# Moving the row fetch between weight pairs, and loading the first pair as two transfers, in a mixture-of-experts decoder step

## The reference

```
proj  = h @ w_in                                  # (tokens, 1024) @ (1024, 3072)
mixed = stick_breaking_attention | differential_attention
x     = layer_norm(ALPHA * x + mixed @ w_out)
logits = x @ w_router + b_router                  # 32 experts
gates  = softmax(top_4(logits))
for the tokens routed to expert e:
    g, u = split(x @ w_gate_up[e] + b_gate_up[e]) # (n, 1024) @ (1024, 2048)
    hid  = (clip(u, -7, 7) + 1) * (min(g, 7) * sigmoid(1.702 * min(g, 7)))
    y   += gate * (hid @ w_down[e] + b_down[e])   # (n, 1024) @ (1024, 1024)
x     = layer_norm(ALPHA * x + y)
```

## Time and profile before

| | |
|---|---|
| median of 3 runs | 1326.35 us (1326.22 to 1326.98) |
| profiled execution, its own time | 1327.01 us |
| its span, first to last instruction | 1325.2 us |
| mean granted TensorE clock | 0.987 |
| PE busy | 1271.4 us (96%) |
| DVE busy | 457.1 us (34%) |
| ACT busy | 260.4 us (20%) |
| moved by DMA | 498.38 MB, mean 376 GB/s |
| PE idle until gate and up weights land (L1815) | 11.5 us |

### The profile page before, as it was taken

How to read it: one execution, slowest core, us unless ns; L and a number is a source line. 1 busy time by engine, 2 the same in 40 slices (tenths; PEclk the granted TensorE clock), 3 DMA queues, 4 the chain that set the end, 5 groups by cost and what they waited for, 6 DMA issues and landing times.

```text
span 1325.2 us, 19517 instructions
## 1 busy us (share of the span) xinstructions
PE 1271.4 (96%) x7682; PEld 514.0 (39%) x7683; DVE 457.1 (34%) x986; ACT 260.4 (20%) x607; POOL 85.5 (6%) x92
## 2 busy tenths in 40 slices
PE   8999997999999999999999999999999999999995
PEld 6354444664433333333333333333333333333332
DVE  1265364775842232222332222233222232222225
ACT  1333345753420110100110100011100110100002
POOL 2023234310010000000000000000000000000000
PEclk9999998999899999999999999999999999999998
DMA  9679779887589999999999995999999999999992
GB/s 367 243 292 355 253 312 372 303 357 256 199 313 409 426 429 428 428 428 427 430 429 428 428 428 234 406 426 428 430 428 428 428 429 428 428 430 429 427 428 93
DMA packets 53308, 498.38 MB, mean 376 GB/s; under 512 B 6793, under 2 KB 7945, under 8 KB 26386
## 3 DMA queue, kind: packets, MB, share of 16 engines
q1 hardware_dynamic: 41586, 430.62, 77.9%
q0 software_dynamic: 11520, 67.11, 13.1%
q10 hardware_dynamic: 160, 0.07, 0.0%
HBM read 493.58 MB, written 3.93 MB: 375 GB/s over the span
## 4 chain that ended last, share of the span: by engine, by line
PE 50%; DMA 23%; ACT 2%; DVE 1%; issue 0%; SPq 0%; ACTq 0%; DVEq 0%
PE psum L1815 25%; DMA arena<-in_w_gate_up 23%; PE psum L1863 11%; PE psum L1461 4%; PE psum L1796 3%; PE psum L1644 2%; PE psum L1476 2%; PE psum L1469 1%; ACT arena L1945 1%; ACT arena L1979 1%; PE psum L1628 1%; PE psum L1667 0%; PE psum L1656 0%; DVE arena L2353 0%; PE psum L1639 0%
## 5 line engine op out<-in xcount | busy, mean ns | idle before, releaser
L1815 PE MATMUL psum<-arena 128*64 128x512 f32 x2112 | 462.2, 593 | 11.5 <-DMA arena<-in_w_gate_up 11.5
L1815 PEld LDWEIGHTS psum<-arena 128*64 128x64 f32 x2112 | 150.4, 137 | 316.0 <-issue 288.4
L1863 PE MATMUL psum<-arena 128*64 128x512 f32 x1056 | 233.9, 595 | 3.3
L2296 DVE TENSOR_SCALAR arena<-psum 128x512 f32<-128x512 f32 x33 | 22.8, 692 | 610.6 <-PE psum L1815 610.6
L1863 PEld LDWEIGHTS psum<-arena 128*64 128x64 f32 x1056 | 72.9, 137 | 150.2 <-issue 131.9
L2243 DVE SCALAR_TENSOR_TENSOR arena<-psum,arena 128x1024 f32<-128x1024 f32 (+1 forms) x96 | 103.3, 1103 | 69.4 <-PE psum L1800 37.2
L1975 ACT ACTIVATE arena<-arena 128x512 f32<-128x512 f32 x32 | 20.2, 630 | 455.4 <-DVE arena L2296 455.4
L1461 PE MATMUL psum<-arena 128*64 128x512 f32 x408 | 95.1, 601 | 0.0
L1191 DVE STREAM_TRANSPOSE arena<-arena 128x1024 f32<-128x1024 f32 x64 | 75.0, 1217 | 1.8 <-DVE arena L1291 0.9
L1796 PE MATMUL psum<-arena 64*128 64x512 f32 x264 | 65.9, 615 | 1.9 <-issue 1.9
L1983 ACT ACTIVATE arena<-psum 128x512 f32<-128x512 f32 x33 | 19.7, 597 | 239.8 <-PE psum L1863 239.8
(11 more groups left out here) (268 smaller groups left out, 1001.0 us busy)
## 6 DMA issues: line engine op xcount, KB each, us to landing
arena<-in_w_gate_up SPq DMA_DIRECT2D x128, 2048.0 KB, 19.6
arena<-in_w_down SPq DMA_DIRECT2D x62, 2048.0 KB, 16.6
arena<-in_w_in SPq DMA_DIRECT2D x12, 1024.0 KB, 11.8
arena<-in_w_out SPq DMA_DIRECT2D x4, 1024.0 KB, 10.6
arena<-in_w_down SPq DMA_DIRECT2D x4, 1024.0 KB, 13.9
arena<-in_x_prompt SPq DMA_DIRECT2D x4, 512.0 KB, 5.0
out<-arena SPq DMA_DIRECT2D x8, 256.0 KB, 6.3
arena<-in_ln_g SPq DMA_DIRECT2D x2, 512.0 KB, 7.6
```

The source lines that it names most:

```text
L1815: ins = nc.tensor.matmul(psum[64 * h:64 * h + 64, n, :], x_k, slot[k][:, col:col + 512], start=False, stop=(k == KD - 1))
L1863: ins = nc.tensor.matmul(psum[64 * h:64 * h + 64, 7, :], h_k, slot[s][:, col:col + 512], start=(k == 0), stop=(k == KD - 1))
```

## The change

The fetch of the next item's rows moves, in every item but item 0, from behind slot 7 to between slot 3 and slot 4. The first pair (slots 0 and 1) becomes two transfers of 1 MB. Each has its own `w_loaded` and `w_used` semaphore; the even rows (8 KB pieces, one for each partition, 16 KB apart in memory) go to slot 0 and the odd rows to slot 1, so each slot holds what it held before. SP issues them in the order 0, 1, 2, 4, 6, 8, 10. The other pairs stay as they are.

```diff
+HALVED = (0,)
-        w_loaded = {s: sem(f"w_loaded{s}") for s in range(0, RING, 2)}
+        w_loaded = {s: sem(f"w_loaded{s}") for s in range(RING) if s % 2 == 0 or s - 1 in HALVED}
             if s < KD:
-                src = a["w_gate_up"][0, bass.ds(e, 1), s * P:(s + 2) * P, :].rearrange("e (p r) n -> (e p) (r n)", r=2)
-                dst = ring[:, s * SLOT:(s + 2) * SLOT]
+                first = s // 2 * 2
+                rows = a["w_gate_up"][0, bass.ds(e, 1), first * P:(first + 2) * P, :]
+                if first in HALVED:
+                    src = rows.rearrange("e (p r) n -> r (e p) n", r=2)[s % 2]
+                    dst = slot[s]
+                else:
+                    src = rows.rearrange("e (p r) n -> (e p) (r n)", r=2)
+                    dst = ring[:, s * SLOT:(s + 2) * SLOT]
@@ SP, before the items
-                load_weights(sp, 0, 0)
+                for s in (0, 1):
+                    load_weights(sp, 0, s)
-        w_used = {s: sem(f"w_used{s}") for s in range(0, RING, 2)}
+        w_used = {s: sem(f"w_used{s}") for s in range(RING) if s % 2 == 0 or s - 1 in HALVED}
+        products_done = w_used[KD - 1 if KD - 2 in HALVED else KD - 2]
@@ SP, expert 1
-                for s in range(0, KD, 2):
-                    sp.wait_ge(w_used[s], done)
-                    load_weights(sp, 1, s)
+                for s in w_used:
+                    if s < KD:
+                        sp.wait_ge(w_used[s], done)
+                        load_weights(sp, 1, s)
@@ SP, experts 2 to 31
-                    for s in range(0, RING, 2):
+                    for s in w_used:
                         sp.wait_ge(w_used[s], done)
                         load_weights(sp, e, s)
@@ PE, body(t)
                     for k in range(KD):
-                        if k % 2 == 0:
+                        if k in w_loaded:
                             pe.wait_ge(w_loaded[k], loaded)
...
-                        if k % 2:
+                        if k in w_used and k // 2 * 2 in HALVED:
+                            ins.then_inc(w_used[k], 1)
+                        elif k % 2:
                             ins.then_inc(w_used[k - 1], 1)
...
-                    fetch(t + 1)
+                        if k == 3 and not first:
+                            fetch(t + 1)
                     if first:
+                        fetch(t + 1)
                         turn_gates()
@@ DVE, body(t)
-                    dve.wait_ge(w_used[KD - 2], t + 1)
+                    dve.wait_ge(products_done, t + 1)
```

## The result

The changed kernel takes 1334.2 us (median of 6 runs, 1332.8 to 1334.59) against 1326.45 for the kernel before. The ratio is 1.0054, 95% interval 1.0041 to 1.0067: 7.2 us slower by that ratio (the two medians lie 7.75 apart), with 5.4 to 8.9 in the interval. The forecast was 1325.8, its range ended at 1329.8. The profiled execution has a span of 1332.6 us, 7.4 more than before.

What follows compares the result with a forecast made beforehand. The prediction took the DMA weight stream to bound two long stretches; -2.76 us from the fetch's move and +2.24 from the halves gave -0.5, so 1326.5 for the profiled execution and a median of 1325.8 us, range 1322.0 to 1329.8.

Steps and rivals of the forecast that it cites:

- Both stretches stay with DMA: In two long runs of weight transfers, DMA still sets the time: 28.78 us an item for PE, below 29.36.
- PE's pace: Items where PE follows itself without waiting for weights: 28.18 us before, forecast 28.78 after the change.
- the double-item expert: The expert with two items, which holds the ring; its last pair lands at 800.87 us and DMA then stands still.
- stretch two: Weight stream after the expert with two items: 89 transfers from slot 8's landing at 851.8 us to 1288.75.
- 0.6 us exposed an item: Behind slot 7, DVE work the fetch used to cover comes into the open: 0.6 us, bounds 0 to 0.75.
- The turn: From the end of gate and up products to the down products: forecast 1.98 us shorter without the fetch.
- 2 us off the last turn: Behind the last weight landing, PE's way to the down products gets shorter by 1.98 us.
- The halves: 0.08 us a pair: First pairs as two transfers in the DMA-bound stream: 28 x 0.08 = +2.2 us (0 to 5.9).
- the early issue: Slot 0 issued 1.7 us earlier through the halved first pair; gain taken 0, at most 1.9 us, twice.
- The rivals: Pieces free, 1323.6 us (0.24); stream pays for halves, 1329.5 (0.2); early issue counts, 1322.0 (0.07); change does nothing, 1328.6 (0.06).
- Rival 2: In both DMA-bound stretches halves cost 0.21 us a pair, 5.9 us in all: net +3.1, 1329.5 us; chance 0.2.
- stretch one: Weight stream from slot 8's issue for expert 2 (415.74 us) through 77 transfers of 4.893 to the landing at 800.8.

Runs made afterwards that it cites:

- the dose: Kernel before plus one or two redundant 128x512 products ahead of each fetch, nothing else: 1318.81 and 1321.51 us against 1305.4, ratios 1.0101 and 1.0120.

## Why the prediction was wrong

- *"Both stretches stay with DMA", since an item at PE's pace of 28.78 us is below 29.36.* This step failed, and it alone gave the wrong sign. Being slower an item is not enough; the stream must be so much slower that PE's lead runs out within the stretch. The rows had it. In the kernel before, PE without waits would come to the fourth pair of the double-item expert at 418.99 + 13 x 28.18 + 10.30 = 795.6, and that lands at 800.8: 5.2 us. In stretch two it is 847.15 + 15 x 28.18 + 10.30 = 1280.2 against 1288.79: 8.6. These 13.9 us are nearly all of the 14.3 that PE waited. An exposure of 0.6 to 0.7 us takes 13 x 0.7 = 9.1 and 15 x 0.7 = 10.5 of it, and the fetch ahead of slot 4 another 2.6 each time. Both stretches go over to PE, and then every one of the 32 exposures is paid, not two. I counted an item's rate against the stream's and named as condition that it stay under 29.36 us; the dose shows that condition to be false.
- *0.6 us exposed an item.* The exposed drain was right; the item is 0.70 longer. The turn is 1.98 us shorter as forecast (the drain at +2.78 where I had 2.9, the transposes at +4.11 where I had 4.2). What was missing is 0.11 us of hand-over: the fetch costs 2.68 us in its new place, where I had subtracted 1.98 from 2.58.
- *The mechanism of the exposure* (DVE's drain behind `hid`, waited for by the transposes) was right: it is in the chain of every item, and moving the wait takes 0.36 of the 0.60 us away.
- *2 us off the last turn.* Right where the last landing decides: -1.7 us in the kernel with only the last item changed. It did not take place in the changed kernel, since no landing decides there.
- *The halves: 0.08 us a pair, no gain from the early issue.* The price is right (0.08 to 0.09 with one pair, 0.08 with four) and it is not paid in the changed kernel, where the fetch alone takes the same 1334.1. The early issue brought nothing, as forecast: with the halves alone slot 8 landed no earlier, at 854.0 us against 851.8. The Trainium skill, DMA: Bandwidth & Descriptors (sections Bandwidth and The descriptor swizzle), gave an estimate of 95 ns, from figures for transfers that GpSimd issues; the trace agrees within 15 ns. The fit of the Trainium skill that I set against the full queue (same page, Anatomy of one DMA) is also for a transfer issued by GpSimd, and the weights are issued by SP, so the trace does not contradict it.
- *The rivals.* None was the one that came. Rival 2, the slower one, had the wrong mechanism. The right one stood only among the conditions at the end, with its threshold too high: not from 1.18 us exposed an item (29.36 - 28.18) does it decide, but from 0.2 in stretch one and 0.4 in stretch two, as worked out above.

## What to carry to other kernels

Where a fast worker runs ahead of a slower stream, compare sums over the stretch, not rates: the worker's work without waits, up to the point where it needs the last piece, against when that piece lands. Their difference is all that the worker can lose before each further item costs its full price. While the stream decides, what a change on the worker can win is the work behind the last landing. Work taken from behind a dependency chain is cover removed: ask what it hid, and fill the stream's waits with the work that itself has a long follow-up (here the scatters, whose drains DVE can do early), not with the work that covers another engine.

## What the runs showed of the hardware

A product on one 64-column half of the array takes as long as one on each half, 0.85 us for 128x512 in float32: one redundant product made items of 29.03 us, two made 29.04, against 28.18 with none. Halving 2 MB transfers from 16 KB to 8 KB pieces costs 0.08 us each in a full queue, 429 GB/s against 424 with all four gate and up pairs halved (windows of 29.4 and 29.5 us). In one run 2.60 us of idle PE ahead of 32 matmul records were followed by a granted clock of 0.50 for some 3 us, and the records took 8.78 us in place of 7.09. And one chip ran the same kernel 21 us faster than another; in the profiles of the kernels run there items have the same pace, and the difference lies ahead of item 0.
